# One ring of nine places for all expert weights, with loops over triples of experts

## What is computed

```python
h = rmsnorm(x, norm_mix_g); proj = h @ w_in
x = x + merged @ w_out
hf = rmsnorm(x, norm_ffn_g)
logits = hf @ w_router + b_router          # top 4 of 32, softmax over them
def expert_block(tok, e):
    gu = x_pad[tok] @ w1[e] + b1[e]        # w1[e]: 1024 x 2048
    gate = minimum(gu[:, :F], 7.0); up = clip(gu[:, F:], -7.0, 7.0)
    act = (up + 1.0) * gate * sigmoid(1.702 * gate)
    return act @ w2[e] + b2[e]             # w2[e]: 1024 x 1024
x = x + sum of gate_weight * expert_block
out = rmsnorm(x, norm_final_g)
```

## Time and profile before

| | before |
|---|---|
| median of 3 runs | 1286.86 us (1283.99 to 1287.0) |
| profiled execution, its own time | 1285.6 us |
| its span in the profile | 1283.8 us |
| busy: PE, PEld, DVE, ACT, POOL | 92%, 47%, 28%, 17%, 4% |
| read from HBM | 460.82 MB |
| chain that ended last | DMA 54%, PE 42%, DVE 2% |

### The profile page before, as it was taken

One profiled execution on the slowest core, in us unless ns is written; L12 is line 12 of the kernel. 1 busy time (PEld: TensorE's weight loads), 2 busy tenths in 40 slices (PEclk: granted clock), 3 DMA queues, 4 the chain that ended last, 5 costly groups with the idle time before them and its releaser, 6 DMA issues.

```text
span 1283.8 us, 17595 instructions
## 1 busy us (share of the span) xinstructions
PE 1180.2 (92%) x7307; PEld 602.7 (47%) x7307; DVE 361.3 (28%) x656; ACT 216.2 (17%) x325; POOL 56.5 (4%) x38
## 2 busy tenths in 40 slices
PE   5999999999799999899999999889999999989897
PEld 5999888998533333333333333333333333333332
DVE  4664754533522211112111111111221121111112
ACT  5444544421600000000000000000000000000001
POOL 0850000000200000000000000000000000000000
PEclk9999999999799999999999999999999999999999
DMA  9754435833399999999999999999999999999995
GB/s 314 254 190 172 178 138 207 335 148 124 155 392 427 430 427 431 427 430 427 429 428 429 429 426 430 427 430 427 431 427 430 427 430 428 429 429 426 430 427 229
DMA packets 56158, 462.31 MB, mean 360 GB/s; under 512 B 5577, under 2 KB 7170, under 8 KB 31586
## 3 DMA queue, kind: packets, MB, share of 16 engines
q1 hardware_dynamic: 52776, 458.58, 86.3%
q10 hardware_dynamic: 3354, 3.33, 0.8%
HBM read 460.82 MB, written 1.07 MB: 360 GB/s over the span
## 4 chain that ended last, share of the span: by engine, by line
DMA 54%; PE 42%; DVE 2%; ACT 1%; issue 0%; SPq 0%; DVEq 0%; ACTq 0%
DMA w_ring<-in_w 54%; PE ps L984 13%; PE ps L782 4%; PE ps L784 4%; PE ps L785 4%; PE ps L1016 2%; PE ps L910 2%; PE ps L791 2%; PE ps L789 2%; PE ps L790 2%; PE ps L905 1%; PE ps L1047 1%; PE ps L918 1%; PE ps L919 1%; PE ps L920 1%
## 5 line engine op out<-in xcount | busy, mean ns | idle before, releaser
L984 PE MATMUL ps<-w_ring,A_W 128*64 128x512 f32 x2048 | 466.3, 599 | 71.4 <-DMA w_ring<-in_w 70.0
L984 PEld LDWEIGHTS ps<-w_ring,A_W 128*64 128x64 f32 x2048 | 137.5, 137 | 363.6 <-issue 232.7
L1016 PE MATMUL ps<-w_ring,A_W 128*64 128x512 f32 x1024 | 232.2, 595 | 1.9 <-DMA w_ring<-in_w 1.8
L1398 DVE TENSOR_SCALAR A_W<-ps 128x512 f32<-128x512 f32 x32 | 22.1, 692 | 517.8 <-PE ps L984 517.8
L1122 DVE TENSOR_TENSOR w_parts<-w_ring,w_parts 128x1024 fp32r<-128x1024 f32 x76 | 105.5, 1398 | 91.4 <-ACT w_parts L553 87.5
L1016 PEld LDWEIGHTS ps<-w_ring,A_W 128*64 128x64 f32 x1024 | 69.7, 136 | 120.3 <-issue 115.6
L711 ACT ACTIVATE A_W<-A_W 128x512 f32<-128x512 f32 x32 | 20.2, 630 | 548.8 <-DVE A_W L1398 548.8
L782 PE MATMUL ps<-hT_hi,w_parts 128*128 128x256 f32 x384 | 109.9, 286 | 2.0 <-DVE hT_lo L1134 2.0
L784 PE MATMUL ps<-hT_lo,w_parts 128*128 128x256 f32 x384 | 109.3, 285 | 0.0
L785 PE MATMUL ps<-hT_hi,w_parts 128*128 128x256 f32 x384 | 109.3, 285 | 0.0
L553 ACT ACTIVATE w_parts<-w_ring 128x1024 fp32r<-128x1024 f32 x76 | 80.0, 1058 | 83.1 <-PE ps L785 53.5
(11 more groups left out here) (204 smaller groups left out, 837.2 us busy)
## 6 DMA issues: line engine op xcount, KB each, us to landing
w_ring<-in_w SPq DMA_DIRECT2D x191, 2048.0 KB, 24.8
w_ring<-in_w_in SPq DMA_DIRECT2D x38, 1024.0 KB, 7.2
w_ring<-in_w_ret_branch SPq DMA_DIRECT2D x2, 2048.0 KB, 13.8
A_W<-in_w_out SPq DMA_DIRECT2D x1, 2560.0 KB, 14.7
xb<-in_x SPq DMA_DIRECT2D x4, 512.0 KB, 3.8
A_QK<-in_w_att_branch SPq DMA_DIRECT2D x1, 2048.0 KB, 12.6
w_ring<-in_w SPq DMA_DIRECT2D x4, 512.0 KB, 8.1
w_ring<-bias_scratch ACTq DMA_DIRECT2D x1, 1536.0 KB, 8.1
```

The lines of the kernel that those rows point to most:

```text
L984: mm = pe.matmul(o, XT[:, k, :], w1_ring[:, k, c * HALF:(c + 1) * HALF], start=(k == 0), stop=(k == KC - 1))
L1016: mm = pe.matmul(ps[CAP * c:CAP * c + CAP, 3, :], lhs, w2_ring[:, q, c * HALF:(c + 1) * HALF], start=False, stop=(q == FQ - 1))
```

## The change

All units pass through one ring of nine places, in the order in which PE uses them. Unit number n goes to place n mod 9, has that place's semaphore (s_unit), and may be loaded when unit n - 9 is used; one counter, s_used, counts the units that PE has used. Six places are the old ones. The three new places lie on memory that was free from some point of the dense part on: behind_merged (on A_PT and gr), behind_xb (on xb and the first 2048 words of A_QK) and behind_gates (on words 2048 to 6143 of A_QK).

So that these can be overwritten, the router tables (chosen, weighed, posm, gates, top, lists, s_w, s_one, mask_f) move from A_QK to A_W, where the expert loop's small tiles move closer together, xs and junk move to the end of A_QK, and the squares' unused output gets a place of its own. The two memsets of POOL (sc_w, y_sb) now wait for the last low part of the tokens.

Eighteen units of three experts are two turns of the ring, so the loops of PE and SP take three experts in one body and run ten times (SP's first turn is written out). DVE's and ACT's loops keep one expert. The waits of DVE for w1_used and w2_used become waits for s_used. The extra rounds for an expert with more than 64 tokens use semaphores of their own.

```diff
+E_UNITS = W1_UNITS + W2_UNITS
+UNIT_WORDS = W1_ROWS * 2 * F
+RING = 9
+TRIPLE = 3
+N_UNITS = N_EXP * E_UNITS
...
+        behind_xb = nc.alloc_sbuf_tensor_at("behind_xb", [P, UNIT_WORDS], F32, offset=nc.sbuf_base - 4 * TT * D)
...
+        behind_gates = nc.alloc_sbuf_tensor_at("behind_gates", [P, UNIT_WORDS], F32, offset=nc.sbuf_base - 4 * 10240 + 4 * 2048)
...
+        behind_merged = nc.alloc_sbuf_tensor_at("behind_merged", [P, UNIT_WORDS], F32, offset=nc.sbuf_base - 4 * 2304)
...
+        ring = [w1_part(1), w1_part(0), w2_part(0), w2_part(1), w1_part(2), w1_part(3),
+                behind_merged[:, :], behind_xb[:, :], behind_gates[:, :]]
...
+        def w1_number(e, u):
+            return u if e == 0 else W1_UNITS + E_UNITS * (e - 1) + u
+
+        def w2_number(e, u):
+            return W1_UNITS + E_UNITS * e + W1_UNITS + u if e < N_EXP - 1 else N_UNITS - W2_UNITS + u
+
+        def place(n):
+            return ring[n % RING], s_unit[n % RING], 16 * (n // RING + 1)
+
+        def load_w1(sp, e, u, n):
+            flat, landed, _ = place(n)
+            sp.dma_start(w1_tile(flat), w1_source(e, u)).then_inc(landed, 16)
...
             sp.wait_ge(s_wl, UNITS * 18)
-            load_w1(sp, main, 0, 1)
+            load_w1(sp, 0, 0, 0)
             sp.wait_ge(s_wl, LAST_UNIT)
-            load_w1(sp, main, 0, 0)
+            load_w1(sp, 0, 1, 1)
...
             sp.wait_ge(s_br, 4)
-            for u in range(W2_UNITS):
-                load_w2(sp, main, 0, u)
-            sp.wait_ge(s_wo, TT)
-            for u in range(2, W1_UNITS):
-                load_w1(sp, main, 0, u)
-            for u in range(W1_UNITS):
-                sp.wait_ge(main.w1_used, u + 1)
-                load_w1(sp, main, 1, u)
-            with sp.Fori(1, N_EXP - 1) as e:
-                for u in range(W1_UNITS):
-                    sp.wait_ge(main.w1_used, e * W1_UNITS + u + 1)
-                    load_w1(sp, main, e + 1, u)
-                for u in range(W2_UNITS):
-                    sp.wait_ge(main.w2_used, e * W2_UNITS - (W2_UNITS - 1 - u))
-                    load_w2(sp, main, e, u)
-            sp.wait_ge(main.w2_used, (N_EXP - 2) * W2_UNITS + 1)
-            load_w2(sp, main, N_EXP - 1, 0)
-            sp.wait_ge(main.w2_used, (N_EXP - 2) * W2_UNITS + 2)
+            load_w1(sp, 0, 2, 2)
+            load_w1(sp, 0, 3, 3)
+            sp.wait_ge(s_wo, TT)
+            for u in range(3):
+                load_w1(sp, 1, u, 4 + u)
+            sp.wait_ge(s_x2, 2 * TT)
+            load_w1(sp, 1, 3, 7)
+            sp.wait_ge(s_x2sq, 2 * TT)
+            sp.wait_ge(s_lg, TT)
+            load_w2(sp, 0, 0, 8)
+            sp.wait_ge(s_used, 1)
+            load_w2(sp, 0, 1, 9)
...
+            with sp.Fori(1, (N_EXP - 2) // TRIPLE) as r:
+                for i in range(TRIPLE):
+                    for u in range(W1_UNITS):
+                        n = w1_number(i + 1, u)
+                        sp.wait_ge(s_used, r * (TRIPLE * E_UNITS) + n - RING + 1)
+                        load_w1(sp, r * TRIPLE + i + 1, u, n)
+                    for u in range(W2_UNITS):
+                        n = w2_number(i, u)
+                        sp.wait_ge(s_used, r * (TRIPLE * E_UNITS) + n - RING + 1)
+                        load_w2(sp, r * TRIPLE + i, u, n)
...
+            sp.wait_ge(s_used, N_UNITS - 2 - RING + 1)
+            load_w2(sp, N_EXP - 1, 0, N_UNITS - 2)
+            sp.wait_ge(s_used, N_UNITS - 1 - RING + 1)
             for j in range(W2_ROWS):
...
+            pool.wait_ge(s_lo, 2 * TT)
             pool.memset(sc_w, 0.0).then_inc(main.swe, 1)
...
+            with pe.Fori(0, (N_EXP - 2) // TRIPLE) as r:
+                rounds = r * (16 * TRIPLE * E_UNITS // RING)
+                for k in range(TRIPLE):
+                    i = r * TRIPLE + k
+                    hidden(i + 1, w1_number(k + 1, 0), rounds)
+                    pe.wait_ge(main.ate, i + 1)
+                    gather(main, i + 2)
+                    scatter(main, i)
+                    pe.wait_ge(main.x, i + 3)
+                    project_down(i, w2_number(k, 0), rounds)
+                    pe.wait_ge(main.swe, i + 2)
+                    transpose_act(main, i + 1)
```

More of the change, by code:

```diff
@@ L974, in gather, with hidden_unit, hidden_bias, hidden @@
                 mm.then_inc(s.gathered, 1)
[L976 to L981, removed]
+            def hidden_unit(flat, u):
+                tile = w1_tile(flat)
+                for j in range(W1_ROWS):
+                    k = u * W1_ROWS + j
                     for c in range(4):
                         o = ps[CAP * (c % 2):CAP * (c % 2) + CAP, c // 2, :]
-                        mm = pe.matmul(o, XT[:, k, :], w1_ring[:, k, c * HALF:(c + 1) * HALF],
+                        mm = pe.matmul(o, XT[:, k, :], tile[:, j, c * HALF:(c + 1) * HALF],
                                        start=(k == 0), stop=(k == KC - 1))
[L986 to L992, removed]
+                return mm
+            def hidden_bias(s, i):
+                pe.wait_ge(s.sel1, i + 1)
+                for c in range(4):
+                    o = ps[CAP * (c % 2):CAP * (c % 2) + CAP, c // 2, :]
+                    pe.matmul(o, sel1[0:BIAS_ROWS, :], bias[:, c * HALF:(c + 1) * HALF], start=False, stop=False)
+            def hidden(i, first, rounds=0):
+                pe.wait_ge(main.x, i + 1)
+                for u in range(W1_UNITS):
+                    flat, landed, count = place(first + u)
+                    pe.wait_ge(landed, rounds + count)
+                    hidden_unit(flat, u).then_inc(s_used, 1)
+                    if u == 0:
+                        hidden_bias(main, i)
+            def hidden_extra(i):
+                pe.wait_ge(extra.x, i + 1)
+                for u in range(W1_UNITS):
+                    pe.wait_ge(s_extra1[u], i * 16 + 16)
+                    hidden_unit(w1_part(u), u).then_inc(extra.w1_used, 1)
+                    if u == 0:
+                        hidden_bias(extra, i)
             def transpose_act(s, i):
@@ L1017, in down_row, with down_unit, project_down @@
                                    start=False, stop=(q == FQ - 1))
                 return mm
-            def project_down(s, i):
-                down_bias(s, i)
+            def down_unit(flat, u):
+                for q in range(u * W2_ROWS, (u + 1) * W2_ROWS):
+                    mm = down_row(flat, q)
+                return mm
+            def project_down(i, first, rounds=0):
+                down_bias(main, i)
                 for u in range(W2_UNITS):
-                    pe.wait_ge(s.w2[u], i * 16 + 16)
-                    for q in range(u * W2_ROWS, (u + 1) * W2_ROWS):
-                        mm = down_row(q)
-                    mm.then_inc(s.w2_used, 1)
+                    flat, landed, count = place(first + u)
+                    pe.wait_ge(landed, rounds + count)
+                    down_unit(flat, u).then_inc(s_used, 1)
@@ L1067, in _ @@
             pe.wait_ge(s_bias, 12)
-            hidden(main, 0)
+            hidden(0, w1_number(0, 0))
             gather(main, 1)
@@ L1094, in _ @@
                     gather(extra, i)
-                    hidden(extra, i)
+                    hidden_extra(i)
                     transpose_act(extra, i)
-                    project_down(extra, i)
+                    project_down_extra(i)
                     scatter(extra, i)
```

159 lines of the change are left out of this document (97 added, 62 removed).

## The result

The kernel with the change takes 1275.16 us (1273.77 to 1276.97, 4 runs), against 1285.63 us before in the same comparison. The medians are 10.5 us apart. The ratio is 0.9916, with a 95% interval from 0.9902 to 0.9931, which is a gain of 8.9 to 12.6 us. The forecast was 1274 us and a gain of 12.4 us. The profiled execution took 1276.97 us, with a span of 1275.1.

What follows compares the result with a forecast made beforehand. The weight stream's start, rate and end were taken to bound the kernel. Gains of 10.6 us at the start and 1.8 us at the end sum to 12.4 us, giving 1273.2 to 1274.5, forecast 1274 us, range 1270 to 1280.

Steps and rivals of the forecast that it cites:

- What bounds the kernel: Whole run: the weight stream's gapless start, its rate and what follows its last byte set the end; PE's waits total 70.0 us.
- PE's first wait: Expert loop, a sign to look for: PE first waits for a weight unit 3.2 experts later, near 570 us.
- The scatter of expert 30: Near the loop's end, a sign: PE's scatter numbered 30, which adds expert 29's result, comes at about 1241.7 us.
- Three more loads: Start of the stream, behind the wait for `w_out`: five loads instead of two fill the empty queue, gaining 10.6 us.
- Nine places in the steady part: Expert loop: more outstanding loads can't make full DMA engines faster, costed at 0, with 2.8 us either way.
- The end: Last expert: its `w2` units are issued eight units early, so PE's wait goes, gaining 1.8 us.
- What costs nothing: Moved router tables, load issues, POOL's later memsets and PE's extra register operations: no cost, being covered by slack.
- The number: Whole kernel: a gain of 10.6 + 1.8 = 12.4 us, forecast as 1274 us.
- rival 1: PE's loop body: fetched again each round beside the stream, 0.6 MB or 1.4 us, giving 1275.7 us; chance 0.08.
- Rival 2: PE's jump back: stalls make PE the bound, from 8.3 us per jump; 1309 us at 12 us each; chance 0.04.
- Rival 3: Start of the stream: gap filled only in part, by one extra unit, gaining 6.7 us, 1280 us; chance 0.06.
- Rival 4: Weight stream: nothing gained, for instance through a stream 1.33% slower; chance 0.03, and 0.01 more that the kernel loses.

## Why the prediction was right, point by point

- **What bounds the kernel.** Right. The stream's start, rate and end set the time, and PE's waits fell from 70.0 to 60.7 us (forecast 59). PE's first wait came at 589 us and not near 570. Stream and PE both began 1.7 us later, which moves it by 1.7 us, and PE's unit at 370.50 us took 5.35 us and not 3.65, in a window whose granted clock was 0.89. A PE that is 1.7 us later needs half an expert more to eat its lead, some 13 us (an estimate from the 3.31 us per expert); the 4 us that are left are open. The scatter of expert 30 came at 1243.97 us and not at 1241.7: 1.7 us of that is the later start, and 0.6 the smaller gain below. None of this changes the end by more than those 0.6 us.
- **Three more loads, 10.6 us.** The mechanism was right, shown by the kernels with none and one of them. The measured size is 10.0 us in the profiled executions; the 0.6 us of difference may be the rounding of the windows' rates or the two more code packets that fall in 330 to 460 us, and weren't told apart.
- **Nine places in the steady part, 0.** Right: 429 GB/s, periods of 29.36 us, and a ratio of 0.9991 with nine places and no load in the gap, which the end's gain alone would put at 0.9984.
- **The end, 1.8 us.** The profile has 2.04 us, 12.54 against 10.50. I had counted from the end of the bias rows, and the next matmul starts 0.17 us ahead of that end: the last expert's bias is at 1256.56 for 0.41 us, and the matmul at 1256.80. Holding the last `w2` back returned 0.9 us of it in the profile and not the 1.8 to 2.0 expected.
- **What costs nothing.** Right for tables, memsets and registers. One cost was missed: the longer program ends in 9.7 to 10.8 us behind the last scatter in most profiles, 1.6 us more in the profiled one. I had costed the code at nothing inside the loop and hadn't asked what it does at its end. With it the sum of the profile's differences is -10.0 - 2.0 + 1.6 = -10.4 us, near the medians' 10.5.
- **The number.** The gain was forecast as 12.4 us and is 10.5 by the medians. The time came nearer, 1275.16 against 1274, with some luck: the forecast started from 1286.86 and 1285.6 us, and the kernel before took 1285.63 in the comparison, from which 12.4 us would lead to 1273.2.
- **Rivals 1 and 2**, a body fetched again each round, did not come about at 984 matmuls and weight loads: there is no packet on q8 between 460 and 1200 us. At 1968 rival 1 came about, and its way of pricing by bytes was too low: 44 packets are 0.7 MB or 1.7 us by bytes, and cost 8.6 us. (Its own time was added up wrong: 1274 and 1.4 us are 1275.4 and not 1275.7.) Rival 2 didn't: the stops of 2.66 to 3.1 us lie far below its 8.3 us per jump. By the Trainium skill (Runtime: NRT & Kernel Launch, Instruction fetch mechanics) a jump outside two pages of 16 KiB fetches; the trace disagrees for the body of 984, some 66 KB by my estimate.
- **Rival 3**, one unit only, has the very time that its kernel had: 6.7 us forecast, 0.9952 or 6.2 us measured. The loads in the change came in time.
- **Rival 4** fell with the windows.

## What to carry to other kernels

Where a transfer stream is the bound, its time is its bytes by its rate plus every stretch in which its queue ran dry; look for these in windows of a few us at the first use, the last load and each change of stage, and don't look for them in the depth of a ring whose engines are full. An extra buffer is worth the time of its load only as far as a gap is there to take it, and the memory for it need only be free from the start of that gap on. Before a loop body is made longer, look at the instruction queue: a body that no longer stays on chip takes time from a full stream even where the engine that runs it has slack.

## What the runs showed of the hardware that was not expected

PE kept a loop body of 984 matmuls and weight loads without fetching it again, and fetched one of 1968 in every round, some ten packets of 16 KB per jump with a stop of 2.7 to 3.1 us. Each such packet cost the full weight stream some 0.2 us, five times its bytes, and the DMA engines then stood half idle for the last 9 us of the stream. One packet of code that meets the output stores goes with 1.0 to 2.5 us more at the end of the run.
